# Two narrow projection blocks: the weights' low halves placed beside the high halves, two products in place of three

## The chip, the cores and the metric

The kernel runs on one core of a Trainium2 chip. Its time is the device time of one execution in microseconds, and the figure for a kernel is the median of its runs. Nothing is computed on the host except the packing of the inputs into tiles.

## The reference

Two blocks follow each other on a sequence of 2048 tokens of width 1024, batch 1. The first is a state-space block with a context of 256 tokens before the sequence, the second a block with a gated linear recurrence beside a forgetting attention. What matters here are their input projections, and one narrow slice of each:

```python
# first block, for the 2048 tokens and for the 256 context tokens
hm = rmsnorm(h, norm_w) * (1.0 + scale) + shift
p = hm @ w_in                       # 1024 x 5152
dt_raw = p[..., OFF_DT:]            # the last N_DIR * SSD_HEADS = 32 columns: time steps
dt = softplus(dt_raw + dt_bias)     # sets the decay of the scan in each direction
...
# second block
proj = h @ w_in[l]
xr, zr, q, k, v, za, fl = jnp.split(proj, split_idx, axis=-1)   # fl: the last 8 columns
log_f = jax.nn.log_sigmoid(fl + b_fgate[l])
d_cum = jnp.cumsum(log_f, axis=1)   # the attention's logits get d_cum of query minus d_cum of key
```

## The kernel before, in words

Every phase is written by hand: each engine has its own program, and semaphores order them. The phases are `front` (norm and projection of the first block), `ssd`, `mix_out`, `projection2`, `attention` and `out2`, with a barrier between most of them.

**The products.** A projection takes a block of 128 columns of the weights at a time. Everything on TensorE is to be precise to more than one rounded value, so each number is split in two, a rounded high half and the remainder, the low half. ScalarE writes the high halves of a block's weights (`high`, L320 and L1506), VectorE the low halves as the difference (`low`, L447 and L1604). The transposed activations lie in SBUF as a high and a low tensor too. For each chunk of 512 tokens and each of the 8 slices of the 1024 input features, TensorE then adds three products in PSUM: high weights by high activations, high weights by low activations, low weights by high activations.

```python
for j, (wt, xx) in enumerate(((w_hi, hi), (w_hi, lo), (w_lo, hi))):
    mm = pe.matmul(PS[:, c, 0:width], wt[n][:, q, :], xx[:, q, cols], ...)
```

**The narrow blocks.** `front` walks over 41 blocks. Blocks 0 to 16 have five chunks, four of 512 tokens and one of the 256 context tokens; blocks 17 to 40 have four. Block 16 is `DT`, the time steps: its weights are 32 real columns and 96 columns of zeros. `projection2` walks over 25 blocks of four chunks, and its first, block 0, is `FL0`, the forget gates, with 8 real columns and 120 of zeros. Both go through the same three products as a full block.

**What follows block DT.** ScalarE copies each chunk from PSUM to SBUF (`evacuate`, L354). While TensorE is at block 17, it turns DT's output to token order (`turn`, L656, 18 tiles in five groups), VectorE copies the groups from PSUM (`read_groups`, L462, only 32 columns of each tile), and SyncE's queue stores them (`store_tok`, L206). The next items of that queue are the load of a table (L261), which waits for that store, and the weights of block 20. VectorE's next work is `pool(17)` (L486 to L502), which waits for the same store; ScalarE can copy block 18's first chunk only when `pool(17)` is done. Block 17 also carries the first of 32 small products (L610) whose weights ScalarE's queue loads (L364). The time steps are read again from block 25 on.

**What surrounds block FL0.** `projection2` begins with eight loads of activations (`load_h`, three buffers), which ScalarE splits (L1510) and VectorE completes (`low_h`, L1610). Chunk `c` of block 0 waits until `2c + 2` of these are done (`pe.wait_ge(S["lo"], 2 * c + 2)`, L1746). ScalarE then copies the 8 rows of each chunk to `acc` (L1530), SyncE stores them to `flT` (L1413) and loads them back at its block 3 as a tile of 128x128 (`fx`, L1468). At block 6 VectorE computes the sums of the forget gates from `fx` (`forget`, L1665 to L1678), between the low halves of blocks 7 and 8; TensorE's one small product for it (L1762) stands behind block 6. `conv(1)` writes over `acc` and waits for the store.

## Time and profile before

| | us |
|---|---|
| median of 3 runs | 3491.55 |
| lowest and highest of them | 3487.11, 3496.17 |
| the profiled execution, its own time | 3487.76 |
| span of the profiled execution, first to last instruction | 3486.1 |
| TensorE busy with matmuls | 3263.6 (94%) |
| VectorE busy | 1637.1 (47%) |
| ScalarE busy | 967.4 (28%) |
| mean share of full speed granted to TensorE's clock | 0.951 |

The profile was taken of one execution. Times of instructions are counted from the start of its span. PE is TensorE, DVE is VectorE, ACT is ScalarE, SPq the queue of SyncE. A matmul's record is longer than its place in the stream, since matmuls overlap; what one costs in a full stream is the distance from its start to the next one's start. L12 is line 12 of the kernel.

### The profile page before, as it was taken

How to read it: one execution, taken by the hardware profiler on the slowest of the kernel's cores; microseconds unless marked ns; L12 is line 12 of the kernel's file. 1: busy time of each engine (PE TensorE's matmuls, PEld its weight loads, DVE VectorE, ACT ScalarE, POOL GpSimd, SP SyncE). 2: the span in 40 equal slices, each digit the busy share in tenths (PEclk: the TensorE clock that was granted, in tenths of full speed). 3: DMA queues.
4: the chain of work that ended last, by engine and by line, in shares of the span. 5: the costliest groups of instructions: out<-in, count | busy, mean ns of one | idle time of the engine just before them, and what ended most of it. 6: DMA issues, size and time to landing. Idle time of an engine off the chain costs nothing. (4 is left out here: it accounts for less than half of the span.)

```text
span 3486.1 us, 37796 instructions
## 1 busy us (share of the span) xinstructions
PE 3263.6 (94%) x15012; PEld 2561.4 (73%) x15012; DVE 1637.1 (47%) x1886; ACT 967.4 (28%) x1798; POOL 384.9 (11%) x246
## 2 busy tenths in 40 slices
PE   7899999997999979996999979999998799999898
PEld 7688888876887857774888867878877455555577
DVE  2754443466014237875444434323424455555365
ACT  2512221111211134541222222242323243433310
POOL 0100000000002125554000000000000201100012
PEclk9999999999999968887999989999999699999899
DMA  4222223342126345544333323222222421220233
GB/s 160 72 79 60 96 88 119 121 151 85 71 101 200 129 145 155 154 145 151 119 111 113 122 104 126 92 95 93 73 84 66 106 61 42 57 48 7 79 130 106
DMA packets 210926, 358.43 MB, mean 103 GB/s; under 512 B 22030, under 2 KB 143502, under 8 KB 202899
## 3 DMA queue, kind: packets, MB, share of 16 engines
q1 hardware_dynamic: 187030, 324.33, 28.9%
q10 hardware_dynamic: 16368, 26.36, 2.2%
q0 software_dynamic: 7392, 5.82, 0.8%
q8 instruction: 98, 1.61, 0.2%
q14 instruction: 38, 0.31, 0.0%
HBM read 234.57 MB, written 121.74 MB: 102 GB/s over the span
## 5 line engine op out<-in xcount | busy, mean ns | idle before, releaser
L636 PE MATMUL p_ps<-hmT_hi,p_w_hi 128*128 128x512 f32 x1312 | 524.4, 400 | 21.5 <-ACT p_work L356 15.9
L636 PE MATMUL p_ps<-hmT_hi,p_w_lo 128*128 128x512 f32 x1312 | 513.6, 391 | 0.0
L636 PE MATMUL p_ps<-hmT_lo,p_w_hi 128*128 128x512 f32 x1312 | 513.1, 391 | 0.0
L1751 PE MATMUL p_ps<-h2T_hi,p_w_hi 128*128 128x512 f32 x800 | 328.1, 410 | 19.3 <-DVE h2T_lo L1610 19.3
L1751 PE MATMUL p_ps<-h2T_hi,p_w_lo 128*128 128x512 f32 x800 | 316.1, 395 | 0.0
L1751 PE MATMUL p_ps<-h2T_lo,p_w_hi 128*128 128x512 f32 x800 | 315.8, 395 | 0.0
L636 PEld LDWEIGHTS p_ps<-hmT_hi,p_w_hi 128*128 128x128 f32 x1312 | 248.1, 189 | 75.5 <-issue 21.1
L636 PEld LDWEIGHTS p_ps<-hmT_hi,p_w_lo 128*128 128x128 f32 x1312 | 247.7, 189 | 53.1
L636 PEld LDWEIGHTS p_ps<-hmT_lo,p_w_hi 128*128 128x128 f32 x1312 | 248.2, 189 | 49.3
L1913 PE MATMUL t_psO<-t_prob,t_v 128*65 128x512 f32 (+3 forms) x640 | 261.0, 530 | 0.9 <-DVE t_out_turned L2023 0.2
L1970 ACT ACTIVATE t_prob<-t_psS 128x1024 f32<-128x1024 f32 (+1 forms) x160 | 150.2, 938 | 307.7 <-PE t_psS L1901 178.1
L2012 DVE TENSOR_REDUCE t_chunk_max<-t_psM 128x1 f32<-128x512 f32 (+2 forms) x320 | 182.1, 606 | 97.7 <-PE t_psM L1884 70.0
L1751 PEld LDWEIGHTS p_ps<-h2T_hi,p_w_hi 128*128 128x128 f32 x800 | 152.9, 191 | 56.8 <-issue 24.5
L462 DVE COPY p_work<-p_ps 128x512 f32<-128x512 f32 (+3 forms) x93 | 55.6, 630 | 295.1 <-PE p_ps L656 260.5
L1751 PEld LDWEIGHTS p_ps<-h2T_lo,p_w_hi 128*128 128x128 f32 x800 | 152.6, 191 | 36.7 <-issue 6.0
L1751 PEld LDWEIGHTS p_ps<-h2T_hi,p_w_lo 128*128 128x128 f32 x800 | 152.7, 191 | 32.8
L1900 PE MATMUL t_psS<-t_QA,t_KA 128*128 128x512 f32 (+1 forms) x320 | 145.4, 454 | 9.7 <-DMA t_QB<-t_max_lo 9.6
L1913 PEld LDWEIGHTS t_psO<-t_prob,t_v 128*65 128x65 f32 x640 | 83.3, 137 | 96.3 <-issue 80.5
L1604 DVE TENSOR_TENSOR p_w_lo<-p_w_raw,p_w_hi 128x1024 fp32r<-128x1024 f32 x25 | 37.4, 1496 | 241.0 <-ACT p_w_hi L1506 241.0
L1884 PE MATMUL t_psM<-t_KM,t_QB 66*128 66x512 f32 (+2 forms) x320 | 131.7, 480 | 19.6 <-DMA t_KB<-scratch_forget 16.1
L447 DVE TENSOR_TENSOR p_w_lo<-p_w_raw,p_w_hi 128x1024 fp32r<-128x1024 f32 x41 | 51.0, 1245 | 162.1 <-ACT p_w_hi L320 162.0
L1901 PE MATMUL t_psS<-t_QB,t_KB 68*128 68x512 f32 (+1 forms) x320 | 120.2, 376 | 0.0
(370 smaller groups left out, 5873.4 us busy)
## 6 DMA issues: line engine op xcount, KB each, us to landing
p_w_raw<-in_w_in SPq DMA_DIRECT2D x66, 512.0 KB, 6.1
p_spare<-in_wada ACTq DMA_DIRECT2D x32, 512.0 KB, 5.5
p_spare<-scratch_xs_tok SPq DMA_DIRECT2D x19, 512.0 KB, 4.4
scratch_xs_tok<-p_work SPq DMA_DIRECT2D x8, 1152.0 KB, 6.1
p_work<-in_wada SPq DMA_DIRECT2D x16, 512.0 KB, 3.5
p_work<-in_x SPq DMA_DIRECT2D x16, 512.0 KB, 3.3
scratch_dT<-p_work SPq DMA_DIRECT2D x8, 1024.0 KB, 5.9
scratch_zpT<-p_work SPq DMA_DIRECT2D x8, 1024.0 KB, 4.0
```

The source lines that it names most:

```text
L447: v.tensor_tensor(w_lo[b % 2][:], w_raw[b % 2][:], w_hi[b % 2][:].bitcast(F32), ALU.subtract).then_inc(S["w_lo"], 1)
L462: v.tensor_copy(tok_of(b)[:, 4 * g:4 * g + cnt, 0:width], tiles(PS[:, bank, :])[:, 0:cnt, 0:width]).then_inc(S["group_read"], 1)
L636: mm = pe.matmul(PS[:, c, 0:width], wt[n][:, q, :], xx[:, q, cols], start=(q == 0 and j == 0), stop=(q == KT - 1 and j == 2))
L1604: v.tensor_tensor(w_lo[b % 2][:], w_raw[b % 2][:], w_hi[b % 2][:].bitcast(F32), ALU.subtract).then_inc(S["w_lo"], 1)
L1751: mm = pe.matmul(ps[:, c, :], wt[n][:, q, :], xx[:, q, c * CH:(c + 1) * CH], start=(q == 0 and j == 0), stop=(q == KT - 1 and j == 2))
L1884: mm = pe.matmul(psM[:, m % 2, 0:w], QB[n][0:KM_ROWS, j * P:(j + 1) * P], KM[n][:, c * CH:c * CH + w], start=True, stop=not edge, skip_gro ...
L1900: pe.matmul(out, KA[n][:, ks], QA[n][:, qs], start=True, stop=False, skip_group_check=True)
L1901: mm = pe.matmul(out, KB[n][:, ks], QB[n][:, qs], start=False, stop=not edge, skip_group_check=True)
L1913: mm = pe.matmul(psO[:, o:CH], va[n][:, kt + e, 0:VD], pt[p % 2][:, e, o:CH], start=(kt + e == 0), stop=(kt + e == 4 * qc + 3), skip_group ...
L1970: act.activation(pt[p % 2][:, :, off:CH], psS[p % 2][:, :, off:CH], ACT.Exp, scale=1.0 / 8).then_inc(S["prob"], 1)
L2012: v.reduce_max(mx[:, j, c:c + 1], psM[:, m % 2, 0:w], axis=AX_X).then_inc(S["first_read"], 1)
```

## The change

In both narrow blocks the low halves of the weights are written into unused columns of the tile that holds the high halves: columns 32 to 63 for the time steps, columns 32 to 39 (`FL_LO = 32`) for the forget gates. The third product is left out there. The product of the tile with the high activations now gives high by high in the lower output rows and low by high in the upper ones, and the product with the low activations gives high by low and also low by low, which was not computed before. The two parts are added later: for the time steps by VectorE after the groups are in token order, for the forget gates by VectorE after both parts have been stored and loaded back.

```diff
                     if b == DT:
+                        sp.wait_ge(S["dt_sum"], 1)
                         dst = a["dt_tok"].rearrange("(t p) c -> p t c", p=P)
                         sp.dma_start(dst, tok[:, 0:TT, 0:NDH]).then_inc(S["tok_out"], 16)
...
-                    v.tensor_tensor(w_lo[b % 2][:], w_raw[b % 2][:], w_hi[b % 2][:].bitcast(F32),
-                                    ALU.subtract).then_inc(S["w_lo"], 1)
+                    if b == DT:
+                        own = w_raw[b % 2][:, :, 0:NDH], w_hi[b % 2][:, :, 0:NDH].bitcast(F32)
+                        v.tensor_tensor(w_hi[b % 2][:, :, NDH:2 * NDH], *own, ALU.subtract).then_inc(S["w_lo"], 1)
+                    else:
+                        v.tensor_tensor(w_lo[b % 2][:], w_raw[b % 2][:], w_hi[b % 2][:].bitcast(F32),
+                                        ALU.subtract).then_inc(S["w_lo"], 1)
...
-                        v.tensor_copy(tok_of(b)[:, 4 * g:4 * g + cnt, 0:width],
-                                      tiles(PS[:, bank, :])[:, 0:cnt, 0:width]).then_inc(S["group_read"], 1)
+                        src = tiles(PS[:, bank, :])
+                        if b == DT:
+                            ins = v.tensor_copy(tok[:, 4 * g:4 * g + cnt, 0:2 * NDH], src[:, 0:cnt, 0:2 * NDH])
+                        else:
+                            ins = v.tensor_copy(tok_of(b)[:, 4 * g:4 * g + cnt, :], src[:, 0:cnt, :])
+                        ins.then_inc(S["group_read"], 1)
+                    if b == DT and gs[-1] == 4:
+                        v.wait_ge(S["group_read"], groups_before(DT + 1))
+                        v.tensor_tensor(tok[:, 0:TT, 0:NDH], tok[:, 0:TT, 0:NDH], tok[:, 0:TT, NDH:2 * NDH],
+                                        ALU.add).then_inc(S["dt_sum"], 1)
...
-                        for j, (wt, xx) in enumerate(((w_hi, hi), (w_hi, lo), (w_lo, hi))):
+                        terms = ((w_hi, hi), (w_hi, lo)) + (((w_lo, hi),) if b != DT else ())
+                        for j, (wt, xx) in enumerate(terms):
...
-                        sp.dma_start(a["flT"][0], acc[0:NH2, :]).then_inc(S["fl_out"], 16)
+                        for part in range(2):
+                            sp.dma_start(a["flT"][part], acc[FL_LO * part:FL_LO * part + NH2, :]).then_inc(S["fl_out"], 16)
...
                     if b == 3:
-                        sp.wait_ge(S["fl_out"], 16)
-                        sp.dma_start(fx, a["flT"].rearrange("o h (s l) -> (o h s) l", l=P)).then_inc(S["fl_in"], 16)
+                        sp.wait_ge(S["fl_out"], 32)
+                        for dst, src in ((fx, a["flT"][0]), (f0, a["flT"][1])):
+                            sp.dma_start(dst, src.rearrange("h (s l) -> (h s) l", l=P)).then_inc(S["fl_in"], 16)
...
-                        act.activation(acc[0:NH2, cols], ps[0:NH2, c, :], ACT.Identity).then_inc(S["read"], 1)
+                        act.activation(acc[0:FL_LO + NH2, cols], ps[0:FL_LO + NH2, c, :], ACT.Identity).then_inc(S["read"], 1)
...
+                    if b == 0:
+                        own = w_raw[0][:, :, 0:NH2], w_hi[0][:, :, 0:NH2].bitcast(F32)
+                        v.tensor_tensor(w_hi[0][:, :, FL_LO:FL_LO + NH2], *own, ALU.subtract).then_inc(S["w_lo"], 1)
...
                 def forget():
-                    v.wait_ge(S["fl_in"], 16)
+                    v.wait_ge(S["fl_in"], 32)
                     v.wait_ge(S["seg_in"], 32)
+                    step(v.tensor_tensor(fx, fx, f0, ALU.add))
...
+                        terms = ((w_hi, x_hi), (w_hi, x_lo)) + (((w_lo, x_hi),) if b >= 1 else ())
                         for q in range(KT):
-                            for j, (wt, xx) in enumerate(((w_hi, x_hi), (w_hi, x_lo), (w_lo, x_hi))):
+                            for j, (wt, xx) in enumerate(terms):
```

## Rows read from the trace of the kernel before

**Rows 1.** The page: busy us, share, instructions; granted clock (tenths) in 40 slices.
```profile
PE 3263.6 (94%) x15012; PEld 2561.4 (73%) x15012; DVE 1637.1 (47%) x1886; ACT 967.4 (28%) x1798; POOL 384.9 (11%) x246
...
PEclk9999999999999968887999989999999699999899
```

**Rows 2.** Waits of TensorE: waiting line, releaser, us in total, times, longest.
```profile
PE p_ps L1751 <- DVE h2T_lo L1610: 19.3, 2, 19.1
...
PE p_psT L1719 <- DVE p_side L1639: 10.9, 3, 4.5
```

**Rows 3.** Timeline of TensorE, block DT: start us, us, line, out<-in.
```profile
539.75 0.39 PE L636 MATMUL p_ps<-hmT_hi,p_w_hi 128*128 128x512 f32 x1
539.98 0.39 PE L636 MATMUL p_ps<-hmT_lo,p_w_hi 128*128 128x512 f32 x1
...
561.28 0.39 PE L636 MATMUL p_ps<-hmT_hi,p_w_lo 128*128 128x512 f32 x1
561.51 0.28 PE L636 MATMUL p_ps<-hcT_hi,p_w_hi 128*128 128x256 f32 x1
...
563.87 0.28 PE L636 MATMUL p_ps<-hcT_hi,p_w_lo 128*128 128x256 f32 x1
```

**Rows 4.** Stretches: us, busy PE, PEld, DVE, ACT, POOL, PEclk, DMA share, GB/s.
```profile
565.00:700.00 135.00, 135.00 (x749) 115.81 (x748) 56.78 (x54) 15.56 (x23) 0.00 (x0) 1.00 0.40 137
2125.00:2560.00 435.00, 435.00 (x1928) 353.31 (x1927) 147.18 (x118) 122.23 (x156) 14.43 (x6) 1.00 0.25 85
```

**Rows 5.** Timeline of VectorE from the end of conv(15) to pool(17).
```profile
549.74 1.22 DVE L447 TENSOR_TENSOR p_w_lo<-p_w_raw,p_w_hi 128x1024 fp32r<-128x1024 f32 x1
...
578.99 0.44 DVE L462 COPY p_work<-p_ps 128x128 f32<-128x128 f32 x2 [7.41 <-PE p_ps L656]
594.47 0.43 DVE L487 MEMSET p_work<- 128x448 f32 x1 [15.04 <-ACT p_work L354]
...
599.87 2.29 DVE L501 TENSOR_TENSOR p_work<-p_work 128x2048 f32<-128x2048 f32 x1
```

**Rows 6.** Timeline of SyncE's queue at the time steps' store.
```profile
579.46 0.37 SPq L206 DMA_DIRECT2D scratch_dt_tok<-p_work  x1
586.07 0.33 SPq L261 DMA_DIRECT2D p_work<-in_inv_count  x1
```

**Rows 7.** Timeline of TensorE, block FL0.
```profile
2096.65 0.77 PE L1751 MATMUL p_ps<-h2T_hi,p_w_hi 128*128 128x512 f32 x1 [19.10 <-DVE h2T_lo L1610]
...
2101.05 0.63 PE L1751 MATMUL p_ps<-h2T_lo,p_w_hi 128*128 128x512 f32 x1
2101.48 0.57 PE L1751 MATMUL p_ps<-h2T_hi,p_w_lo 128*128 128x512 f32 x1
2101.89 0.39 PE L1751 MATMUL p_ps<-h2T_hi,p_w_hi 128*128 128x512 f32 x1
...
2115.31 0.39 PE L1751 MATMUL p_ps<-h2T_hi,p_w_lo 128*128 128x512 f32 x1
2115.86 0.50 PE L1751 MATMUL p_ps<-h2T_hi,p_w_hi 128*128 128x512 f32 x1 [0.16 <-DVE h2T_lo L1610]
```

**Rows 8.** Timeline of VectorE, low halves of activations 4, 6, 8, then weights.
```profile
2101.42 2.29 DVE L1610 TENSOR_TENSOR h2T_lo<-p_side,h2T_hi 128x2048 fp32r<-128x2048 f32 x1 [2.35 <-ACT h2T_hi L1510]
...
2107.51 2.29 DVE L1610 TENSOR_TENSOR h2T_lo<-t_k_raw,h2T_hi 128x2048 fp32r<-128x2048 f32 x1 [1.26 <-ACT h2T_hi L1510]
...
2113.51 2.29 DVE L1610 TENSOR_TENSOR h2T_lo<-t_q_raw,h2T_hi 128x2048 fp32r<-128x2048 f32 x1 [0.56 <-ACT h2T_hi L1510]
2115.72 1.22 DVE L1604 TENSOR_TENSOR p_w_lo<-p_w_raw,p_w_hi 128x1024 fp32r<-128x1024 f32 x1
```

**Rows 9.** Stretches with the granted clock (PEclk, third from the end).
```profile
66.00:90.00 24.00, 11.02 (x42) 8.79 (x43) 21.95 (x43) 17.48 (x41) 5.21 (x5) 1.00 0.27 88
1450.00:1500.00 50.00, 50.00 (x211) 35.98 (x210) 43.05 (x23) 26.08 (x87) 26.68 (x15) 0.90 0.54 169
1500.00:1550.00 50.00, 50.00 (x201) 37.16 (x201) 37.02 (x22) 24.11 (x80) 26.34 (x18) 0.83 0.48 152
2563.00:2566.00 3.00, 0.69 (x5) 0.69 (x6) 2.96 (x4) 0.60 (x1) 0.00 (x0) 1.00 0.00 0
2566.00:2569.00 3.00, 3.00 (x9) 2.28 (x8) 2.91 (x3) 0.00 (x0) 0.00 (x0) 0.51 0.00 0
```

**Rows 10.** Timeline of VectorE in forget(): first step, last before TensorE, next.
```profile
2236.75 0.29 DVE L1668 TENSOR_SCALAR p_side_last<-p_side_last,f_bias 128x128 f32<-128x128 f32 x1
...
2243.55 0.17 DVE L1672 COPY f_ends<-p_side_last 128x2 f32<-128x2 f32 x1
2252.34 0.16 DVE L1674 COPY f_offsets<-p_psG 128x1 f32<-128x1 f32 x1 [8.63 <-PE p_psG L1762]
```

More of the change, by code:

```diff
@@ L160, in front @@
                            "tok_out", "act_out", "raw_out", "d_out", "inv_in", "half_used", "grow", "g_out", "b_in",
-                           "mod2", "dt_in", "ask", "exp", "adt", "acum", "acum_read", "wst_ready", "r_turned", "r_hi", "r_lo",
+                           "mod2", "dt_sum", "dt_in", "ask", "exp", "adt", "acum", "acum_read", "wst_ready", "r_turned", "r_hi", "r_lo",
                            "dec_out", "weighted", "summed", "state"))
@@ L446, in low @@
                         v.wait_ge(S["chunk"], chunks_before(b - 1))
-                    v.tensor_tensor(w_lo[b % 2][:], w_raw[b % 2][:], w_hi[b % 2][:].bitcast(F32),
-                                    ALU.subtract).then_inc(S["w_lo"], 1)
+                    if b == DT:
[4 more added lines that the diff above has]
+                                        ALU.subtract).then_inc(S["w_lo"], 1)
                 def read_groups(b, gs):
-                    width = NDH if b == DT else P
                     for g in gs:
@@ L634, in product @@
                     for q in qs:
-                        for j, (wt, xx) in enumerate(((w_hi, hi), (w_hi, lo), (w_lo, hi))):
+                        terms = ((w_hi, hi), (w_hi, lo)) + (((w_lo, hi),) if b != DT else ())
+                        for j, (wt, xx) in enumerate(terms):
                             mm = pe.matmul(PS[:, c, 0:width], wt[n][:, q, :], xx[:, q, cols],
-                                           start=(q == 0 and j == 0), stop=(q == KT - 1 and j == 2))
+                                           start=(q == 0 and j == 0), stop=(q == KT - 1 and j == len(terms) - 1))
                     if qs[-1] == KT - 1:
@@ L1341, in projection2 @@
     host = lambda u: 8 + 2 * u
+    FL_LO = 32
     unit_at = lambda b: (b - 8) // 2 if 8 <= b <= 22 and b % 2 == 0 else None
@@ L1603, in low @@
                         v.wait_ge(S["chunk"], 4 * (b - 1))
-                    v.tensor_tensor(w_lo[b % 2][:], w_raw[b % 2][:], w_hi[b % 2][:].bitcast(F32),
-                                    ALU.subtract).then_inc(S["w_lo"], 1)
+                    if b == 0:
+                        own = w_raw[0][:, :, 0:NH2], w_hi[0][:, :, 0:NH2].bitcast(F32)
+                        v.tensor_tensor(w_hi[0][:, :, FL_LO:FL_LO + NH2], *own, ALU.subtract).then_inc(S["w_lo"], 1)
+                    else:
+                        v.tensor_tensor(w_lo[b % 2][:], w_raw[b % 2][:], w_hi[b % 2][:].bitcast(F32),
+                                        ALU.subtract).then_inc(S["w_lo"], 1)
                 def low_h(u):
@@ L1619, in conv @@
                     if b == 1:
-                        v.wait_ge(S["fl_out"], 16)
+                        v.wait_ge(S["fl_out"], 32)
                     else:
@@ L1748, in _ @@
                             pe.wait_ge(S["read"], 4 * (b - 1) + c + 1)
+                        terms = ((w_hi, x_hi), (w_hi, x_lo)) + (((w_lo, x_hi),) if b >= 1 else ())
                         for q in range(KT):
-                            for j, (wt, xx) in enumerate(((w_hi, x_hi), (w_hi, x_lo), (w_lo, x_hi))):
+                            for j, (wt, xx) in enumerate(terms):
                                 mm = pe.matmul(ps[:, c, :], wt[n][:, q, :], xx[:, q, c * CH:(c + 1) * CH],
-                                               start=(q == 0 and j == 0), stop=(q == KT - 1 and j == 2))
+                                               start=(q == 0 and j == 0), stop=(q == KT - 1 and j == len(terms) - 1))
                         mm.then_inc(S["chunk"], 1)
@@ L2367 @@
            "x1": [SEQ, D], "h2": [SEQ, D],
-           "xcT": [4, P, SEQ], "zrT": [4, P, SEQ], "qkT": [8, P, SEQ], "va_tok": [SEQ, 2 * W2], "flT": [1, NH2, SEQ],
+           "xcT": [4, P, SEQ], "zrT": [4, P, SEQ], "qkT": [8, P, SEQ], "va_tok": [SEQ, 2 * W2], "flT": [2, NH2, SEQ],
            "forget": [NH2, 2, SEQ], "hzT": [4, P, SEQ]}
```

## The prediction

> **What bounds the kernel now.** I read the busy shares first: TensorE is busy for 3263.6 us of a span of 3486.1 us, twice as long as VectorE [rows 1]. Such a share is an average, so the next view is the stretches around the two blocks that change. From 565 to 700 us, right behind block DT, and from 2125 to 2560 us, behind block FL0, TensorE is busy for the whole stretch at a granted clock of 1.00 [rows 4]. There a matmul that goes away brings everything behind it forward by its place in the stream. Then I read what TensorE waits for: block DT has no entry in its list of waits, but line 1751 waits 19.3 us for the low halves of the activations, nearly all of it before the first matmul of block FL0 [rows 2]. So the two blocks differ. DT lies in a stream that TensorE alone paces; FL0 lies where the activations are still arriving, and part of what it loses there was waiting time in disguise.
>
> **Block DT, matmuls.** Removed are 8 matmuls in each of five chunks, 32 with 512 columns and 8 with 256. In the stream a 512-column matmul costs 0.227 us: from 539.75 to 561.51 us there are 96 starts, 21.76 / 96 [rows 3]. A 256-column one costs 0.118 us: from 561.51 to 563.87 us there are 20 starts, and three more follow to make the chunk's 24 [rows 3]. The sum is 32 x 0.227 + 8 x 0.118 = 7.25 + 0.94 = **8.2 us**, all of it on TensorE's path, since its stream is full before and behind.
>
> Here a rule of the Trainium skill gives another size. The rows show 0.227 us from start to start at full clock. "TensorE: Matmul & The Clock Gate", section "Back-to-back issue gap", gives the columns divided by 2.4 GHz plus about 2.5 ns, which is 0.216 us for 512 columns; by that estimate DT would give 7.8 us and the whole forecast would be smaller by half a microsecond. The trace does not agree with it, and the row is taken.
>
> Does anything else hold back block 17? It would now start at 564.2 - 8.2 = 556 us. Its low weights are ready at 549.74 + 1.22 = 550.96 us [rows 5], 5 us before. The low half of DT's own weights shrinks to a quarter of the elements, on a VectorE that is not waited for there: nothing. ScalarE's copies of DT's chunks 0 to 2 still wait for conv(15) at about 549.8 us, and are done some microseconds before 556. Everything later (the turns, the copies, the loads for the small products) hangs on TensorE's progress and moves with it.
>
> **The time steps' output.** Each copy takes 64 columns of a tile in place of 32; two copies took 0.44 us [rows 5], so at most 0.2 us more each, and in front of them VectorE was idle for 7.41 us. The addition is new: 18 x 32 = 576 elements a partition; the full 2048-element addition took 2.29 us [rows 5], so 0.64 us, between 0.3 us (a step of 128x128) and 1.2 us (one of 1024 elements) as bounds. The store, the load of the table and block 20's weights stand behind it in SyncE's queue and are later by about 0.9 us against TensorE. The table's load was issued at 586.07 us, when the store had landed [rows 6], and pool(17) began at 594.47 us, released by ScalarE's last copy [rows 5]: the store has 8.4 us to spare, and the table itself is used at 599.87 us. Cost 0. If this cover were gone, pool(17) would be late by what exceeds 8.4 us, and ScalarE's first copy of block 18 behind it.
>
> **Block FL0, matmuls.** Removed are 4 x 8 matmuls of 512 columns, 7.3 us at 0.227 each. But each chunk waits for two more low halves. Before, chunk 0 started at 2096.65 us with the clock at half: 0.43 us a matmul until 2101.89 us, twelve of them, then 0.23 [rows 7]. Now it has 16: it ends at 2101.89 + 4 x 0.23 = 2102.8 us. Chunk 1 needs the low half that ends at 2101.42 + 2.29 = 2103.71; chunk 2 the one that ends at 2109.80; chunk 3 the one at 2115.80 us [rows 8]. These ends are set by loads, by ScalarE's split and by three buffers, and none of them waits for TensorE, so they stay. At 16 x 0.227 = 3.6 us each, chunk 1 then runs 2103.8 to 2107.4, chunk 2 2109.9 to 2113.5, and chunk 3 starts at 2115.86 us, exactly as before [rows 7]. Three of the four chunks give their saving to waiting: about 0.9, 2.4 and 2.3 us of idle TensorE. Only the last one's remains: 8 x 0.227 = **1.8 us**. Late next would be block 1's low weights, ready at 2115.72 + 1.22 = 2116.94 us [rows 8], while chunk 3 ends at about 2119.5 us: no new wait. The low half of FL0's own weights is shorter, but VectorE then waits for ScalarE anyway: nothing. Bounds of the term: 0 if a lower clock eats it (below), 7.3 us if the waits were not there.
>
> **The forget gates' output.** ScalarE copies 40 rows in place of 8 at the same number of elements a row: nothing. SyncE has one store and one load more, a microsecond of its queue at blocks 0 and 3, where it has nothing due. VectorE's addition is a step of 128x128, 0.29 us by the step next to it [rows 10]. The scan's end waited 8.6 us for TensorE [rows 10], so 0.3 us more is covered; without that cover it would be 0.3 us on TensorE's path before block 7. Cost 0.
>
> **Sum.** 8.2 + 1.8 = 10.0 us less. Against the profiled execution's own 3487.76 us this is 3477.8 us; against the median of 3491.55 us it is 3481.5 us. The profiled execution stands 3.8 us below that median, which is itself between runs 9 us apart. A measurement of this kernel can tell about 0.3%, 10.5 us, from no change, and 10.0 us lies just inside that.
>
> **The rivals.**
>
> *The clock falls in FL0's new gaps.* At 2563 us TensorE was idle for 2.3 of 3 us, and in the next 3 us, fully busy, it was granted 0.51 of full speed, 1.2 GHz [rows 9]. The gaps before chunks 2 and 3 are as long. Against it: between 66 and 90 us TensorE was busy for less than half the time and kept 1.00 [rows 9]. A fall during chunk 2 costs nothing, as 2.3 us of waiting absorb it; one that covers chunk 3 costs 8 matmuls of 0.43 in place of 0.23, 1.6 us. The result is 8.2 + 1.8 - 1.6 = 8.4 us less, 3483.1 us. The Trainium skill's page on TensorE ("TensorE: Matmul & The Clock Gate", "HAM oscillation") speaks for it, saying that pauses between short groups of matmuls bring the half clock back; by that rule the gain of FL0 is nearly all lost, and the trace agrees in one place and not in the other.
>
> *The low halves come earlier.* If ScalarE or the loads were held back by what TensorE reads, all of FL0's 7.3 us could come out: 8.2 + 7.3 = 15.5 us less, 3476.0 us. For it speaks only that the loads run beside TensorE; against it that each low half follows a split that waits for a load.
>
> *Slower: the clock of the scan stage.* From 1450 to 1550 us TensorE is busy without a break at granted clocks of 0.90 and 0.83, so it spends a fifth to a third of the time at half clock [rows 9]. Three slices of 87 us, 261 us together, have the digit 8 there [rows 1]. Every instruction in them now comes 8.2 us earlier against whatever decides the clock. At a mean of 0.85 they hold 261 x 0.85 = 222 us of work at full clock. To end 0.3% slower the stage has to cost 10.5 + 10.0 = 20.5 us more, 222 us of work in 281.5 us, a mean clock of 0.79: that is the point from which it decides. At 0.78 it takes 284.6 us, 23.6 us more, and the kernel 3481.5 + 23.6 = 3505.1 us. Nothing in the change favours it, and the three runs before, all with this stage, lie within 9 us.
>
> *The change does less than it says.* If the removed matmuls were hidden by weight loads, nothing would go. Weight loads are busy 73% [rows 1] and matmuls start every 0.227 us, so no.
>
> **How the numbers follow.** The full sum, 10.0 us less: 0.57. The clock in the gaps, 8.4 us less: 0.30. Earlier low halves, 15.5 us less: 0.07. Slower: 0.03. Not doing what it says, no change: 0.03. The likeliest gives 3481.5 us. Runs scatter by 4.5 us about their median, so a median of a few runs by perhaps 3; the range takes in 3476.0 less half of that scatter, and the other cases plus the scatter: 3474 to 3488. Faster by over 0.3%, beyond 10.5 us: nearly half of the first case (0.27), a third of the second (0.09), most of the third (0.06), together 0.42. Slower 0.03. The rest, 0.55, is within 0.3%.
>
> **What would show it.** In the profile after: matmuls of block DT start at the same 0.227 us and number 80, not 120; block 17 starts about 8.2 us earlier and pool(17) is still released by ScalarE; between 565 and 700 us TensorE shows no new wait. In block FL0 TensorE waits three times for line 1610's successor, about 0.9, 2.4 and 2.3 us, and block 1 begins 1.8 us less behind the last low half. The granted clock in those 25 us decides between the first two cases. I would be wrong if the low halves ended at other times against block FL0's start, if VectorE's addition released pool(17), or if a phase behind the change took other time than before by more than 2 us.

## The result and the profile after

| | before | changed |
|---|---|---|
| median, us (6 runs each, one session) | 3489.33 | 3468.18 |
| lowest and highest | 3484.89, 3496.17 | 3463.15, 3476.43 |
| profiled execution, its own time | 3487.76 | 3466.3 |
| span | 3486.1 | 3464.3 |

The ratio is 0.9941, with a 95% interval of 0.9924 to 0.9957: 20.6 us less, twice the 10.0 us that were forecast, and below the range. (Of the distance between the forecast time, 3481.5 us, and the 3468.2 us measured, 2.2 us are the base: the forecast stood on the median of three runs of the kernel before, 3491.55 us, and six runs have 3489.33.) The page of the changed kernel, the lines that answer to [rows 1]:

```profile
PE 3244.8 (94%) x14940; PEld 2547.3 (74%) x14940; DVE 1636.4 (47%) x1888; ACT 966.1 (28%) x1798; POOL 385.8 (11%) x246
...
PEclk9999999999999978897999999999999699999899
```

There are 72 matmuls and 72 weight loads fewer, as the diff says, and the granted clock dips in the same places but one (the 24th slice, 8 before and 9 now). Shares say nothing of where 20 us went. For that I laid the two traces beside each other at transfers that both kernels issue, and took the difference of their start times:

| SyncE's queue issues | before | changed | difference |
|---|---|---|---|
| the time steps' store (L206, now L207) | 579.5 | 572.6 | -6.9 |
| the last store of the scan's stage | 1606.3 | 1596.7 | -9.6 |
| `projection2`'s first load | 2083.9 | 2076.3 | -7.6 |
| its first `xcT` store (block 1) | 2152.6 | 2143.9 | -8.7 |
| its first `va_tok` store | 2545.6 | 2536.9 | -8.7 |
| its last `va_tok` store | 2725.8 | 2705.5 | -20.3 |
| the last store of the output | 3483.0 | 3461.2 | -21.8 |

Up to 2540 us the kernel is about where the forecast has it. Such a difference between two single traces is no better than their scatter, though: the stretch from the time steps' store to the last store of the scan's stage took 1026.9 us before and 1024.1 us here, and between 1021.8 us (e5, second trace) and 1032.7 us (e6) over the sixteen traces of this study, though no edit touches it. Then, within the last blocks of `projection2` and where the diff touches nothing, 11.6 us go in one piece: the stretch between the first and the last `va_tok` store took 180.2 us and takes 168.6 us. I call this stretch **the last blocks**.

**Block DT.** The timeline of TensorE in the changed kernel, with the columns of [rows 3]:

```profile
540.05 0.39 PE L649 MATMUL p_ps<-hmT_hi,p_w_hi 128*128 128x512 f32 x1
540.28 0.39 PE L649 MATMUL p_ps<-hmT_lo,p_w_hi 128*128 128x512 f32 x1
540.50 0.39 PE L649 MATMUL p_ps<-hmT_hi,p_w_hi 128*128 128x512 f32 x1
...
556.32 0.28 PE L649 MATMUL p_ps<-hcT_lo,p_w_hi 128*128 128x256 f32 x1
556.44 0.40 PE L649 MATMUL p_ps<-hmT_hi,p_w_hi 128*128 128x512 f32 x1
```

The third product is gone (no row has `p_w_lo`), the distance is still 0.227 us, and block 17 starts at 556.44 us. VectorE and SyncE's queue behind it, which answer to [rows 5, 6]:

```profile
571.12 0.62 DVE L468 COPY p_work<-p_ps 128x256 f32<-128x256 f32 x2 [7.27 <-PE p_ps L669]
571.77 0.76 DVE L474 TENSOR_TENSOR p_work<-p_work 128x576 f32<-128x576 f32 x1
586.60 0.43 DVE L499 MEMSET p_work<- 128x448 f32 x1 [14.06 <-ACT p_work L355]
```

```profile
572.61 0.37 SPq L207 DMA_DIRECT2D scratch_dt_tok<-p_work  x1
578.81 0.33 SPq L262 DMA_DIRECT2D p_work<-in_inv_count  x1
```

The addition is there (0.76 us), the table's load is issued 7.8 us before `pool(17)` begins, and ScalarE's copy still releases `pool(17)`.

**Block FL0.** The rows of TensorE that had to wait, one for each chunk, with the idle time and its end in brackets:

```profile
2089.15 0.76 PE L1773 MATMUL p_ps<-h2T_hi,p_w_hi 128*128 128x512 f32 x1 [19.20 <-DVE h2T_lo L1630]
...
2095.91 0.50 PE L1773 MATMUL p_ps<-h2T_hi,p_w_hi 128*128 128x512 f32 x1 [1.42 <-DVE h2T_lo L1630]
...
2102.01 0.50 PE L1773 MATMUL p_ps<-h2T_hi,p_w_hi 128*128 128x512 f32 x1 [2.18 <-DVE h2T_lo L1630]
...
2109.01 0.50 PE L1773 MATMUL p_ps<-h2T_hi,p_w_hi 128*128 128x512 f32 x1 [1.47 <-DVE h2T_lo L1630]
```

Before there was one such wait inside the block, 0.16 us [rows 7]. The clock in the same stretch, with the columns of [rows 9]:

```profile
2099.00:2102.00 3.00, 0.83 (x4) 0.37 (x2) 2.72 (x2) 1.99 (x2) 0.00 (x0) 1.00 0.82 258
2102.30:2105.60 3.30, 3.30 (x9) 2.57 (x9) 2.29 (x1) 1.13 (x2) 0.00 (x0) 0.52 1.08 303
2105.60:2109.00 3.40, 1.94 (x8) 1.21 (x6) 2.34 (x2) 3.40 (x5) 0.00 (x0) 0.96 0.40 135
2109.00:2113.00 4.00, 3.99 (x17) 3.31 (x18) 1.09 (x1) 0.04 (x2) 0.00 (x0) 1.00 0.00 0
```

**The last blocks.** Each of them stores the output of the block before (1 MB to `scratch_va_tok`, L1424) and only then, as the next item of SyncE's queue, loads the weights of the block after next (L1402). ScalarE's `high` (L1506) waits for that load. These are the two queues at the same block, before and then changed:

```profile
2605.12 0.39 SPq L1424 DMA_DIRECT2D scratch_va_tok<-p_side  x1
2605.61 1.73 SPq L1402 DMA_DIRECT2D p_w_raw<-in_w_in  x1
```

```profile
2593.39 0.39 SPq L1439 DMA_DIRECT2D scratch_va_tok<-p_side  x1
2593.87 1.71 SPq L1416 DMA_DIRECT2D p_w_raw<-in_w_in  x1
```

and ScalarE's wait for that load before, which ends when it has landed:

```profile
2614.03 1.06 ACT L1506 ACTIVATE p_w_hi<-p_w_raw 128x1024 fp32r<-128x1024 f32 x1 [8.08 <-DMA p_w_raw<-in_w_in]
```

The traffic in the 12 us around that load before (first line: busy tenths of the DMA engines in 40 slices, second: GB/s; then by queue, and us from issue to landing):

```profile
DMA  0000000888899999988899899989999996110000
GB/s 0 0 0 0 0 0 12 263 292 287 292 287 294 294 282 294 220 157 176 172 265 376 341 410 423 382 369 410 369 396 410 410 423 260 68 55 27 27 27 27
...
q8 instruction: 1, 0.02, 0.6%
...
p_w_raw<-in_w_in SPq DMA_DIRECT2D x1, 512.0 KB, 8.4
```

and in the 11 us around the same load in the changed kernel:

```profile
DMA  0000000029999999999988999999999999999410
GB/s 0 0 0 0 0 0 0 0 86 302 283 292 294 289 287 292 294 287 261 175 158 177 188 229 412 402 432 387 462 387 447 387 447 343 402 372 462 194 75 30
...
p_w_raw<-in_w_in SPq DMA_DIRECT2D x1, 512.0 KB, 6.6
```

Same transfers, but before there is one packet more, of a queue that the page calls `instruction`, and behind the full rate a tail at 55 and 27 GB/s. The full rate is about 410 GB/s here, an estimated 26 GB/s for each of the 16 engines, so the tail is one or two engines that are not done when the others are, and the load waits for them. Such packets come about every 30 us here. Four intervals between them in the changed kernel, 2557 to 2671 us, are 28.3 us on average (24 to 33 us), and at 753 matmuls and 751 weight loads in 168.6 us that is 252 instructions of TensorE for each. "Runtime: NRT & Kernel Launch", section "Instruction fetch mechanics", in the Trainium skill, says that an engine's instructions come in blocks of 16 KB or 256, through a DMA queue that its sequencer drives; these rows agree.

What the late load costs, in the rows of VectorE that follow it, before:

```profile
2615.13 1.23 DVE L1604 TENSOR_TENSOR p_w_lo<-p_w_raw,p_w_hi 128x1024 fp32r<-128x1024 f32 x1 [10.04 <-ACT p_w_hi L1506]
2618.54 0.69 DVE L1643 TENSOR_SCALAR t_k_raw<-t_k_raw 128x1024 f32<-128x1024 f32 x1 [2.19 <-ACT p_side_last L1557]
2619.27 6.55 DVE L1644 RECIPROCAL t_k_raw<-t_k_raw 128x1024 f32<-128x1024 f32 x1
2625.86 1.29 DVE L1639 COPY p_side<-p_psT 128x512 f32<-128x512 f32 x2
```

`high` releases `low` and ScalarE's roots, these release the 6.55 us reciprocal, and behind it stands the copy that makes room in PSUM for TensorE's next turns. TensorE then waits, before and changed:

```profile
2626.61 0.66 PE L1719 MATMUL p_psT<-ident,p_acc 128*128 128x128 f32 x4 [4.06 <-DVE p_side L1639]
```

```profile
2613.11 0.66 PE L1740 MATMUL p_psT<-ident,p_acc 128*128 128x128 f32 x4 [2.30 <-DVE p_side L1659]
```

The two stretches of the last blocks as a whole, same columns as above:

```profile
2545.60:2725.80 180.20, 165.99 (x753) 132.92 (x751) 66.36 (x56) 52.46 (x62) 7.19 (x3) 0.95 0.30 91
```

```profile
2536.90:2705.50 168.60, 160.68 (x753) 129.66 (x751) 66.26 (x56) 52.56 (x62) 7.19 (x3) 0.98 0.32 97
```

The work is the same, 753 matmuls. TensorE was idle for 180.20 - 165.99 = 14.2 us and is idle for 7.9 us; and the same matmuls were busy 5.3 us longer, at a mean clock of 0.95 in place of 0.98. So of the 11.6 us, 6.3 are waits and 5.3 are half clock.

### The profile page after: what moved, and what is told of

Its sections match the earlier page's. It is cut to its first block and busy times, and to the rows that moved or that the text cites. A ratio compares the mean times of both kernels' runs of the same rounds, so it can differ in the third digit from the quotient of the medians.

```text
span 3464.3 us, 37657 instructions
## 1 busy us (share of the span) xinstructions
PE 3244.8 (94%) x14940; PEld 2547.3 (74%) x14940; DVE 1636.4 (47%) x1888; ACT 966.1 (28%) x1798; POOL 385.8 (11%) x246
## 5 line engine op out<-in xcount | busy, mean ns | idle before, releaser
L649 PE MATMUL p_ps<-hmT_hi,p_w_lo 128*128 128x512 f32 x1280 | 502.7, 393 | 0.0
L1773 PE MATMUL p_ps<-h2T_hi,p_w_lo 128*128 128x512 f32 x768 | 300.8, 392 | 0.0
L470 DVE COPY p_work<-p_ps 128x512 f32<-128x512 f32 (+1 forms) x88 | 54.3, 651 | 282.4 <-PE p_ps L669 246.1
L1773 PEld LDWEIGHTS p_ps<-h2T_hi,p_w_lo 128*128 128x128 f32 x768 | 144.9, 189 | 30.8
```

Of the source, the lines that this page charges most:

```text
L470: ins = v.tensor_copy(tok_of(b)[:, 4 * g:4 * g + cnt, :], src[:, 0:cnt, :])
L1773: mm = pe.matmul(ps[:, c, :], wt[n][:, q, :], xx[:, q, c * CH:(c + 1) * CH], start=(q == 0 and j == 0), stop=(q == KT - 1 and j == len(ter ...
```

## The experiments

The question is what took the last blocks' time away. Theories: **(A)** the larger `flT` moved the scratch tensors behind it to other addresses; **(B)** the kernel arrives there 8.7 us earlier, against something that runs by its own clock; **(C)** the 144 instructions that TensorE has fewer move its instruction fetches against the blocks, and they no longer fall into the weight loads; **(D)** beside (C), whatever delays these loads, it costs only because the load stands behind the store in SyncE's queue. Comparisons are with runs of the kernel before in the same session, whose medians lay between 3486.0 and 3488.7 us. The edits are shown in part, with `...` for what is left out. The time of the last blocks is always that of one traced execution, the median that of all runs.

**e1: the kernel before, `flT` twice as large.**

```diff
-"flT": [1, NH2, SEQ]
+"flT": [2, NH2, SEQ]
...
```

> The kernel before, with only the scratch tensor flT made twice as large, so that the tensors behind it in memory (forget, hzT) lie where they lie in the changed kernel; no instruction is added or removed. Theory of the instruction fetches (TensorE's instructions are fetched in packets of 16 KB; in the kernel before, four of these fell into a weight load that ScalarE waits for, at 2579, 2610, 2640 and 2671 us, and in the changed kernel none): no change, within 3 us of before, weight loads of the last blocks still 7.9 to 8.9 us to landing. Theory of the addresses (the stores and loads of the last blocks are quicker at other places in memory): about 10 us faster than before and weight loads of 6.5 us.

Measured: 3486.91 us (11 runs), ratio 1.000 [0.9989, 1.0011]. The last blocks took 180.4 us and the loads landed as late as before. (A) falls.

**e2 and e3: one half of the change each.** e2 has the change's block DT and the earlier block FL0, e3 the reverse:

```diff
-terms = ((w_hi, x_hi), (w_hi, x_lo)) + (((w_lo, x_hi),) if b >= 1 else ())     # e2, against the changed kernel, projection2
+terms = ((w_hi, x_hi), (w_hi, x_lo), (w_lo, x_hi))
-terms = ((w_hi, hi), (w_hi, lo)) + (((w_lo, hi),) if b != DT else ())          # e3, against the changed kernel, front
+terms = ((w_hi, hi), (w_hi, lo), (w_lo, hi))
...
```

> Only block DT has two products, block FL0 has three as before. Simple theory (each part gives its removed matmuls, the rest of the measured gain belongs to one of them or to chance): 8.2 us faster than before, or 20 less the share of FL0. Theory of the instruction fetches: 80 instructions fewer on TensorE move the fetches of the last blocks by 80/256 of a period of some 30 us, 9 us later against the blocks, out of the weight loads: 8.2 + 10 = 18 us faster, and no fetch during the weight loads of the last five blocks, which land in 6.5 to 6.7 us.

> Only block FL0 has two products, block DT has three as before. Simple theory: 1.8 us faster than before, which nobody could tell from no change. Theory of the instruction fetches: 64 instructions fewer move the fetches about 7.5 us later against the last blocks, out of the weight loads: 1.8 + 10 = 12 us faster, weight loads of 6.5 us. The two parts alone then sum to 30 us, 9 us more than both together gave, which the simple theory excludes.

Measured: e2 3472.0 us, 0.9958 [0.9944, 0.9972], last blocks 169.8 us; e3 3471.28 us, 0.9951 [0.9937, 0.9964], last blocks 171.3 us. Either half alone brings nearly the whole gain of the last blocks. The two gains, 14.6 and 17.1 us by their ratios, add up to 31.7, not to 20.6, so most of each is one and the same saving. Neither total hit its number: 18 us were expected of e2 and 12 of e3. e2's trace has an explanation (its activations came late, below), but e3's 17.1 us (12.5 to 22 by its interval) are some 6 to 7 us more than its last blocks and block FL0 give, and its traced execution, at 3480.5 us, is 9 us above its own median; where the other runs gained that stays open. e3 arrives at the last blocks only 2.4 us earlier than before and gets 8.9 us there; that already speaks against (B). Two traces below settle it: the second of e5 arrives there within 0.3 us of the kernel before and takes 172.4 us, the third arrives 5.0 us later and takes 169.1 us.

**e4: the changed kernel with 144 empty instructions on TensorE** at the head of its program in `projection2`.

```diff
+                for _ in range(144):
+                    pe.nop().then_inc(pad, 1)
                 for b in range(NB):
...
```

> The changed kernel with 144 empty instructions on TensorE at the start of the second projection, where it waits 19 us for the activations: as many as the change removed there and before (72 matmuls and their 72 weight loads). Nothing else differs. Simple theory: no change against the changed kernel, 21 us faster than before, or up to 1 us less. Theory of the instruction fetches: the fetches of the last blocks are back in the weight loads, which land in 7.9 to 8.9 us again, and the gain falls to about 10 us against before.

Measured: 3483.98 us (12 runs), 0.999 [0.9981, 0.9998]; last blocks 181.9 us. The gain there is gone, with every matmul of the change still left out and the arrival still 2.6 us ahead of before. The total was expected 10 us below before and is only 3.5 us below (0.7 to 6.6). The load of the same block as above, from its issue at 2603.28 us:

```profile
GB/s 0 0 0 0 0 17 280 287 292 290 292 288 288 290 287 218 157 171 174 273 382 369 410 369 396 410 410 355 369 423 423 396 246 14 27 27 27 27 27 27
...
q8 instruction: 1, 0.02, 1.3%
...
p_w_raw<-in_w_in SPq DMA_DIRECT2D x1, 512.0 KB, 9.4
```

The fetch is back in the load, and so is the tail. The empties are not free: `projection2`'s beginning, from the first load to the first `xcT` store, took 70.7 us in place of 67.6, because the first matmul comes 22.0 us behind the first load and not 12.9. Last blocks and this together are 13.3 + 3.1 = 16.4 us; the medians, of two sessions, differ by 15.8.

**e5 and e9: the kernel before with 64 and with 112 empty instructions**, in the same place. If the fetches decide, *adding* work to TensorE should make the last blocks faster, since it moves the fetches out of the loads to the other side.

> The kernel before with 64 empty instructions added on TensorE at the start of the second projection, some 7 us inside a wait of 19 us. All matmuls of before are there. Theory that any shift of the instruction fetches out of the weight loads is enough: the fetches of the last blocks come 64/256 of 30 us, 7 us earlier, before the loads they fell into; weight loads land in 6.5 to 6.7 us and the kernel is 10 us faster than before, though it only has more instructions. Theory that the removed work gives the time: no change, or up to 7 us slower.

> The kernel before with 112 empty instructions at the same place: 112 more and 144 fewer are the same phase, as one fetch brings 256 instructions. Theory of the fetches: the fetches of the last blocks lie against the loads as in the changed kernel, the stretch from the first to the last store of va_tok takes 169 to 171 us in place of 180, and the kernel is 8 to 10 us faster than before (the empty instructions take 12 us, some 2 us more than TensorE has to wait there). Theory that the removed work gives the time: no change or slower.

Measured: e5 3483.64 us (12 runs), 0.9997 [0.9987, 1.0006]; e9 3480.97 us (12 runs), 0.9985 [0.9972, 0.9997]. In the last blocks both did what (C) says, 171.0 and 173.3 us, with the loads landing in 6.4 to 6.7 us. The totals were a miss. e9's is accounted for: its first matmul came 16.9 us behind the first load in place of 12.8, the beginning of `projection2` took 71.9 us in place of 68.7, and -6.9 + 3.2 = -3.7 us is near the 5.2 of its ratio. e5's is not: its 64 empties are hidden (the first matmul came at 13.0 us), and yet its beginning took 70.1 us. Two more traces of it:

> A second look at the kernel before with 64 empty instructions, whose profile showed the last blocks at 171 us and 3477.7 us in all, while its median was 3483.6 us. If the fetches stay out of the loads each time, the last blocks take 171 us again and the rest of the difference lies in other stages; if their place changes from run to run, this look can show 180 us.

> A third look at the same kernel, for the same question: 171 us or 180 us for the last blocks, and which stage holds the rest.

Measured: 3485.12 and 3485.39 us, last blocks 172.4 and 169.1 us, all loads in 6.4 to 6.8 us. The gain of 8 to 11 us is there each time. Of what is lost elsewhere one part can be read: the beginning of `projection2`, 71.5 and 70.2 us (before 68.7). The last of the eight activation loads and a fetch, first in the kernel before, then in e5:

```profile
t_q_raw<-scratch_h SPq DMA_DIRECT2D x1, 1024.0 KB, 5.3
...
q8 instruction: 1, 0.02, 0.8%
...
t_q_raw<-scratch_h SPq DMA_DIRECT2D x1, 1024.0 KB, 7.0
```

In all three traces of e5 a fetch starts 1.6 to 1.8 us behind the issue of this load, which then takes 7.0 to 7.2 us, and the last low half of the activations is ready 33.2 to 33.5 us behind the first load, not 31.9. So the empties moved the fetches out of the last blocks and one of them into a load that TensorE waits for at the beginning: the same mechanism with the other sign. (In the second trace the granted clock was also 0.50 for 3.4 us behind the wait for this low half, 1.5 us more.) A fetch is not the only thing that delays this load: it took 8.2 us in e2, with none of TensorE's fetches in it. The rest is within what single traces scatter by. The attention took 536.0 and 535.2 us (534.4 before, 533.8 to 536.2 over the sixteen traces) and the last stage 219.7 and 219.4 (216.4 before, but 218.8 in e1, which has the same instructions, and 215.2 to 222.3 over the sixteen). What loses the 5 to 7 us by which e5's median lies above what its last blocks and its beginning give stays open.

The fetches and loads of all these kernels stand in one table. "Position" is the start of a fetch near the load less the issue of the load, for the last five loads.

| kernel | position of the fetch, us | load, issue to landing, us | last blocks |
|---|---|---|---|
| before | -1.2, 4.8, 4.6, 4.8, 4.6 | 6.7, 7.9, 8.4, 7.9, 8.9 | 180.2 |
| e1 | -1.3, 4.7, 4.6, 4.8, 4.6 | 6.6, 7.9, 8.1, 7.9, 9.2 | 180.4 |
| e4 | -1.2, 1.5, 4.6, 4.8, 4.6 | 6.5, 7.1, 9.4, 7.9, 8.8 | 181.9 |
| changed | 20.1, 15.4, 20.2, 16.8, 20.3 | 6.5, 6.5, 6.6, 6.5, 6.5 | 168.6 |
| e2 | 8.4, 12.2, 8.8, 12.1, 11.1 | 6.6, 6.5, 6.5, 6.4, 6.6 | 169.8 |
| e3 | 8.4, 7.1, 8.6, 12.8, 8.1 | 6.5, 6.5, 6.5, 6.5, 6.7 | 171.3 |
| e5 | -8.2, -5.0, -6.8, -5.1, -5.8 | 6.7, 6.5, 6.5, 6.4, 6.5 | 171.0 |
| e9 | -13.4, -8.5, -12.6, -8.0, -12.3 | 6.7, 6.5, 6.7, 6.5, 6.6 | 173.3 |
| e10 (below) | 8.5, 12.2, 8.7, 12.6, 11.0 | 6.5, 6.5, 6.6, 6.5, 6.5 | 171.2 |

Of the 45 loads in it, the 12 with a fetch 1.5 to 4.8 us behind their issue took 7.1 to 9.4 us, and the other 33 took 6.4 to 6.7 us. (C) holds.

**e10: the changed kernel with 64 empties**, which leaves the fetches outside the loads.

> The changed kernel with 64 empty instructions: the control for what such instructions cost by themselves. The fetches of the last blocks, 15 to 20 us behind the issue of a weight load in the changed kernel, come 7 us earlier, 8 to 12 us behind it, when the load has landed. Theory of the fetches: no change against the changed kernel, 18 to 21 us faster than before, the last blocks 169 to 171 us. If empty instructions cost time by their number: 64/144 of 17, some 7 us slower than the changed kernel.

Measured: 3476.34 us (6 runs), 0.9961 [0.9945, 0.9976]; last blocks 171.2 us. The last blocks held, but the whole lost more than expected. In the profiled execution the 10.4 us above the changed kernel's are 2.6 in the last blocks, 1.5 at the beginning of `projection2` (a half clock in block FL0, below) and 6.7 in the last stage: 222.2 against 215.5 us, near the two ends of what that stage took in the sixteen traces. As with e5, the median is above what the parts with a known cause give.

**e6 and e7: the load ahead of the store**, in the kernel before and in the changed one, for the last blocks only. The load never needed the store: it waits for ScalarE (`high`) and VectorE (`low`) to be done with its buffer.

```diff
                 for b in range(NB):
+                    if b > first_vz and b + 2 < NB:
+                        load_w(b + 2)
                     if b >= 1:
                         store(b - 1)
-                    if b + 2 < NB:
+                    if b <= first_vz and b + 2 < NB:
                         load_w(b + 2)
```

> The kernel before, where SyncE issues the weights of block b + 2 ahead of the store of block b - 1 instead of behind it, for the last blocks of the second projection only. If the chain is store, weight load, ScalarE's high halves, roots, VectorE's decays, copies of the groups, TensorE's turns, as I read it, then ScalarE no longer waits for these loads, and with the 12.9 us of waits and three stretches of half clock that followed goes the whole cost of the late loads: the last seven blocks take 159 us in place of 180, the kernel is 20 us faster than before. If the chain is another (TensorE's own pace), no change.

> The changed kernel with the same early issue of the weight loads. Theory of the fetches: the last blocks take the same 159 us as in the kernel before with the early issue, as neither has a load in the chain; 10 us less than the changed kernel, 30 us less than before. The distance to the kernel before with the early issue is then the change's own worth, 8.2 + 1.8 = 10.0 us, and not 20. If the change itself speeds the last blocks in some other way, the distance stays near 20 us.

Measured: e6 3466.3 us (5 runs), 0.9942 [0.993, 0.9955]; e7 3463.01 us (5 runs), 0.9932 [0.9919, 0.9945]. The last blocks took 158.2 us in both. e6 is the 20 us faster that were expected; e7 is 24 us below before and not 30, and the two are 3.3 us apart where 10 were expected, a miss that e11 and e12 take up. e6 has every matmul of the kernel before, and still this stretch:

```profile
2530.00:2700.00 170.00, 170.00 (x811) 137.88 (x811) 69.36 (x53) 55.68 (x66) 7.21 (x3) 1.00 0.30 90
```

No wait and no half clock. A load and the `high` that uses it, from SyncE's queue and ScalarE's timeline of e6:

```profile
2614.30 0.38 SPq L1402 DMA_DIRECT2D p_w_raw<-in_w_in  x1
```

```profile
2630.41 1.05 ACT L1508 ACTIVATE p_w_hi<-p_w_raw 128x1024 fp32r<-128x1024 f32 x1
```

The load goes out as soon as its buffer is free, 16 us before its use, and `high` waits for nothing. Loads still meet fetches (the one issued at 2578.99 us took 7.8 us), and it costs nothing. (D) holds.

**e8: e7 with 144 empties.**

> The changed kernel with the early issue and with the 144 empty instructions that cost the changed kernel 17 us. Theory of the fetches: a fetch can still fall into a weight load, but nothing waits for it any more, so within 3 us of the same kernel without the empty instructions. If the empty instructions cost time by themselves, 17 us slower than that one again.

Measured: 3465.3 us (5 runs), 0.9935 [0.9923, 0.9948], last blocks 158.2 us. With the loads out of the chain the fetches' place no longer matters; the 2.3 us above e7 are again the empties' own start (70.4 us against 67.8).

**e11 and e12: e6 and e7 once more**, in another session.

> The kernel before with the early issue once more, beside the changed kernel with it on the same chip. If the change's own worth is the sum of its two terms, 8.2 and 1.8 us, this kernel is 10 us slower than the other, and the 3.3 us between their medians so far (five runs each, spread over 10 us) were scatter. If the change costs something elsewhere, the distance stays at 3 us. Last blocks 158 us.

> The changed kernel with the early issue once more. 10 us faster than the kernel before with it if the two terms are all; about 3 us if something else takes 7 us back, which the stages of the two profiles should then show outside block DT and block FL0. Last blocks 158 us.

Measured: e11 3466.61 us (6 runs), 0.9938 [0.9922, 0.9955]; e12 3457.11 us (5 runs), 0.9911 [0.9893, 0.9929]. e7 and e12 are the same kernel, the fastest of the study and faster than both given ones: 24 and 31 us below the kernel before. The pairs also price the change without the last blocks: e6 and e11 together have a mean of 3467.4 us over 11 runs, e7 and e12 of 3460.5 us over 10, a difference of 6.9 us with a standard error of 1.6. (In the first session they were 3.3 us apart, in the second 9.5.)

## Why the prediction was right and wrong

- **Block DT, matmuls: right.** 24.5 us (539.75 to 564.2) became 16.4 us (540.05 to 556.44), 8.1 us where the term had 8.2. Block 17 starts at 556.44 us where "about 556" was said.
- **The time steps' output: right.** Two copies took 0.62 us, 0.18 more than before; the addition took 0.76 us where 0.64 was estimated. The store came 6.9 us earlier, 8.1 less the 0.3 us by which DT started later and less 0.9 of copies and addition. `pool(17)` was still released by ScalarE, and TensorE is busy for all of the stretch that [rows 4] show:

```profile
565.00:700.00 135.00, 135.00 (x742) 114.89 (x742) 55.62 (x51) 15.28 (x23) 0.00 (x0) 1.00 0.42 149
```

- **Block FL0, matmuls: right in kind and in size.** The three gaps were 1.42, 2.18 and 1.47 us, 5.1 together, where 0.9, 2.4 and 2.3 were forecast, 5.6. From the end of the last low half to ScalarE's `high` of block 2 it was 2122.16 - 2115.80 = 6.36 us and is 2113.47 - 2108.95 = 4.52 us: 1.84 less, where the term had 1.8. The low halves themselves ended 0.7 us later against the first load (32.6 us behind it, not 31.9), so at block 1 the stage is only 1.1 us ahead. The other traces say scatter: with the change's block FL0 the last low half was ready at 31.2 (e3), 31.3 (e12) and 32.8 us (e7), without it at 31.6 (e6, e11) to 35.0 us (e2).
- **The rival of the falling clock: it happened, at no cost in this execution, and at its full cost in others.** The clock went to 0.52 behind the gap of 2.18 us, in chunk 2, and the waiting after it took that up, as the text said it would; behind 1.42 and 1.47 us it stayed. Chunk 3 ran at full clock. That was luck. Of the five traces with the gaps of the change's block FL0 (changed, e3, e7, e10, e12) two are like this; in e3, e10 and e12 the longest gap, 2.77, 2.92 and 2.55 us, lay before chunk 3 and the half clock in it:

```profile
2111.26 0.50 PE L1775 MATMUL p_ps<-h2T_hi,p_w_hi 128*128 128x512 f32 x1 [2.55 <-DVE h2T_lo L1632]
...
2112.80:2116.10 3.30, 3.30 (x9) 2.57 (x8) 0.00 (x0) 0.00 (x0) 0.00 (x0) 0.50 0.00 0
```

  From the last low half to `high` of block 2 it is 4.5 us in the changed kernel and e7, 6.1 us in these three and 6.3 to 6.4 us with three products (before, e1, e6, e11). So the half clock took 1.6 us, the rival's price, and of block FL0's 1.8 us 0.2 was left. Three of five is more than the chance of 0.30 that it was given. The rule of the Trainium skill that the text weighed for this rival ("TensorE: Matmul & The Clock Gate", "HAM oscillation") is thus borne out behind one of the three gaps in each of these five traces.
- **The forget gates' output: nothing visible**, as forecast.
- **The two blocks' sum: near.** It was 10.0 us; 8.7 are there at block 1 in the traces, and 6.9 (standard error 1.6) between the kernels with early loads. At `projection2`'s first load, ahead of block FL0, the seven traces with the change's block DT stand at 2076.9 us on average and the nine without it at 2084.1 us, 7.2 us apart.
- **What failed is the premise behind the sum, that all that comes later hangs on TensorE's progress "and moves with it".** The text says it of block DT and takes it for the whole. The prediction named it as a way to be wrong ("if a phase behind the change took other time than before by more than 2 us"), but gave it no rival, no price and no room in the range. It had the rows to ask: the 10.9 us of waiting for the turns' copies [rows 2] and the half clock behind such a wait at 2566 us [rows 9]. I used the second only as evidence for another place and never followed the first to its source. It ends in a 512 KB load that takes 6.5 us when undisturbed, and 7.9 to 8.9 us in four of the five last blocks. So that wait was longer than its work, and something outside the diff decided by how much. e4 shows that this something is the number of TensorE instructions ahead, and e6 that the load's place in the queue is what makes it count.

The sum that fits the traces is 8.7 us at block 1 and 11.6 us in the last blocks, 20.3 us of the 20.6. That it fits to 0.3 us is luck, as the 20.6 us have an interval of 15 to 27 us and the arrival scatters by several; the 11.6 us themselves are firm, since the last blocks took 180.2 to 181.9 us in all three traces with fetches in the loads and 168.6 to 173.3 us in all eight without them and with the load behind the store. Open is why the medians of e5 and e10 lie some 3 to 7 us above what their last blocks and their start of `projection2` give, and that of e3 some 6 to 7 us below.

## What to carry to other kernels

Before a sum is made, every sizeable wait behind the change is followed to its source; where that is a transfer, its time from issue to landing is compared over the blocks, and if it varies for the same bytes, the wait can move by itself and belongs in the range. A change that only alters the *number* of instructions can gain or lose as much as the work it removes; empty instructions in the same number tell the two apart. And a load with nothing to wait for does not belong behind a store in one queue: moving it was worth 20 us here, as much as the whole change, and made the last blocks deaf to the rest. And a difference between two single traces says something only of a stretch that takes the same time in other traces of the same instructions: the last stage, 216.4 us in one and 218.8 in another, is none.

## What the runs showed of the hardware

A fetch of TensorE's instructions (one packet of 16 KB, about one per 28 us in these blocks) shares the DMA engines with data. When it began 1.5 to 4.8 us behind the issue of a 512 KB load, which itself follows a 1 MB store, the load landed in 7.1 to 9.4 us in place of 6.4 to 6.7. The delay is about the time that the fetch's own packet takes on its engine: the four loads whose packet took 2.1 to 2.6 us landed in 8.8 to 9.4 us, the eight whose packet took 0.9 to 1.3 us in 7.1 to 8.4 us (in the rows of e4 above, 1.3% of 16 engines over 12 us is 2.5 us, and the load took 9.4; before, 0.6% is 1.2 us, and it took 8.4). Why one packet of 16 KB takes 0.9 us and another 2.6 us no run shows. The Trainium skill ("Runtime: NRT & Kernel Launch", "Instruction fetch mechanics") calls the cost of crossing into the next block of instructions mostly hidden. TensorE indeed shows no wait of its own for it in the last blocks, where its waits are all for other engines; but the load that it delays is not hidden.

What came ahead of a half clock was not what I had thought either. In the last blocks of the kernel before, the granted clock fell to half five times: behind waits of 2.3, 4.1 and 4.5 us for the turns' copies, and, less expected, 2 to 3 us behind two waits of only 1.0 us (ending at 2587.18 and 2648.47 us, L1731 for ScalarE's sigmoid). The first of the five is at 2566 us in [rows 9]; the second, third and fifth:

```profile
2590.00:2593.00 3.00, 3.00 (x8) 2.33 (x9) 0.00 (x0) 0.00 (x0) 0.00 (x0) 0.50 0.00 0
...
2627.50:2631.00 3.50, 3.50 (x10) 2.68 (x10) 3.40 (x4) 0.00 (x0) 0.00 (x0) 0.51 0.00 0
2689.00:2692.00 3.00, 3.00 (x9) 2.31 (x8) 2.93 (x3) 0.00 (x0) 0.00 (x0) 0.50 0.00 0
```

The changed kernel has three long waits there, of 2.17, 2.30 and 2.16 us, and none for the sigmoid. The clock fell behind the first two and not behind the third:

```profile
2614.30:2617.60 3.30, 3.30 (x10) 2.51 (x9) 3.20 (x4) 0.00 (x0) 0.00 (x0) 0.52 0.00 0
...
2669.00:2672.00 3.00, 2.32 (x12) 2.00 (x13) 2.97 (x4) 0.00 (x0) 0.00 (x0) 1.00 0.02 5
```

So a wait of 1.0 us was followed by half clock twice, one of 2.16 us was not, and in block FL0 those of 1.42 and 1.47 us were not. The length of a wait alone does not tell it here. Slice by slice, the two stretches at half clock in the changed kernel and the five before cost 1.7 us each (a stretch of 3.4 us at half speed). Three fewer are 5.1 us, nearly all of the 5.3 us of busy time that the same 753 matmuls needed less.
